# The last fixed expert's loads in a hybrid decoder layer: waiting for the issue of the first gather instead of its landing

## What is computed

```python
h = rms_norm(x, norm_ffn_gain[l])
...
group_p = softmax(t @ w_router_group + b_router_group)
gp, gi = lax.top_k(group_p, 1)
sel = take_along_axis(exp_logits, gi)
ev, ei = lax.top_k(softmax(sel), TOP_K)      # two experts of one group
for e in range(N_EXPERTS):
    hid = silu(t @ w_expert_gate[e]) * (t @ w_expert_up[e])
    out = out + combine[:, e:e + 1] * (hid @ w_expert_down[e])
```

## Time and profile before

| what | us |
|---|---|
| median of 3 runs | 771.15 (770.96 to 771.22) |
| the profiled execution's own time | 771.41 |
| its span, first to last instruction | 769.7 |
| start of the first gather on POOL | 485.13 |
| first transposition of gathered rows on PE | 492.10 |
| last down product on PE starts | 739.71 |

### The profile page before, as it was taken

How to read it: one execution, slowest core, us unless ns; L and a number is a source line. 1 busy time by engine, 2 the same in 40 slices (tenths; PEclk the granted TensorE clock), 3 DMA queues, 4 the chain that set the end, 5 groups by cost and what they waited for, 6 DMA issues and landing times.

```text
span 769.7 us, 10989 instructions
## 1 busy us (share of the span) xinstructions
PE 699.7 (91%) x4246; PEld 512.5 (67%) x4246; DVE 335.4 (44%) x615; ACT 292.1 (38%) x537; POOL 199.5 (26%) x171
## 2 busy tenths in 40 slices
PE   4999999998999999999999996699999999997940
PEld 3688888887887798888777885454445555454520
DVE  4349897989776422465479136600000000000008
ACT  6322656473354643654544033021222222222123
POOL 2044443332151141433453000212122221211110
PEclk9999999999999999999999997699999999999985
DMA  7904333040030030214941248999999999999827
GB/s 232 339 39 164 110 110 109 2 151 15 14 138 14 1 111 2 70 42 165 381 145 57 77 169 342 376 374 394 418 399 418 396 419 397 419 417 419 339 95 280
DMA packets 45330, 164.66 MB, mean 214 GB/s; under 512 B 9500, under 2 KB 13612, under 8 KB 32478
## 3 DMA queue, kind: packets, MB, share of 16 engines
q1 hardware_dynamic: 39966, 155.52, 52.4%
q0 software_dynamic: 5312, 8.42, 3.1%
HBM read 154.09 MB, written 19.53 MB: 226 GB/s over the span
## 4 chain that ended last, share of the span: by engine, by line
PE 83%; DVE 5%; ACT 4%; issue 3%; DMA 2%; POOL 1%; DVEq 0%; SPq 0%; POOLq 0%; ACTq 0%
PE bank L970 14%; PE bank L472 13%; PE bank L474 13%; PE bank L473 13%; PE bank L1004 7%; PE bank L967 5%; PE bank L945 3%; PE bank L998 2%; PE bank L600 2%; PE bank L981 2%; PE bank L863 1%; PE bank L631 1%; PE bank L621 1%; PE bank L803 1%; PE bank L788 1%
## 5 line engine op out<-in xcount | busy, mean ns | idle before, releaser
L1264 POOL TENSOR_TENSOR w_lo<-arena,w_hi 128x1024 fp32r<-128x1024 f32 x36 | 86.1, 2396 | 211.5 <-ACT w_hi L1427 211.5
L472 PE MATMUL bank<-h_hi,w_hi 128*128 128x512 f32 x320 | 128.3, 401 | 0.4 <-DVE arena L1977 0.4
L474 PE MATMUL bank<-h_hi,w_lo 128*128 128x512 f32 x320 | 125.0, 391 | 0.0
L473 PE MATMUL bank<-h_lo,w_hi 128*128 128x512 f32 x320 | 124.6, 389 | 0.0
L970 PE MATMUL bank<-arena 128*64 128x256 f32 x896 | 105.6, 390 | 7.9 <-issue 7.1
L970 PEld LDWEIGHTS bank<-arena 128*64 128x64 f32 x896 | 65.1, 140 | 38.3 <-issue 8.5
L2344 DVE TENSOR_TENSOR arena<-arena,bank 64x256 f32<-64x256 f32 x28 | 11.5, 412 | 180.1 <-ACT arena L1778 180.1
L1889 DVE SCALAR_TENSOR_TENSOR bank<-arena,bank 128x512 f32<-128x512 f32 x116 | 78.7, 749 | 0.1
L1388 POOL DMA_INDIRECT y_rows<-arena,row_half x28 | 28.0, 1000 | 165.0 <-ACT arena L1799 153.5
L474 PEld LDWEIGHTS bank<-h_hi,w_lo 128*128 128x128 f32 x320 | 60.1, 188 | 13.1
L472 PEld LDWEIGHTS bank<-h_hi,w_hi 128*128 128x128 f32 x320 | 60.1, 188 | 12.9 <-DVE arena L1977 0.6
(11 more groups left out here) (361 smaller groups left out, 1136.6 us busy)
## 6 DMA issues: line engine op xcount, KB each, us to landing
arena<-in_w_expert_down_dram SPq DMA_DIRECT2D x33, 1024.0 KB, 20.6
arena<-in_w_expert_gate_dram SPq DMA_DIRECT2D x33, 1024.0 KB, 17.9
arena<-in_w_expert_up_dram SPq DMA_DIRECT2D x33, 1024.0 KB, 21.6
arena<-in_w_in_dram SPq DMA_DIRECT2D x8, 2048.0 KB, 8.1
arena<-in_x_dram SPq DMA_DIRECT2D x8, 512.0 KB, 7.6
arena<-in_w_in_dram SPq DMA_DIRECT2D x4, 1024.0 KB, 10.6
y_rows<-arena SPq DMA_DIRECT2D x8, 512.0 KB, 10.1
arena<-in_w_out_dram SPq DMA_DIRECT2D x2, 2048.0 KB, 11.0
```

The lines of the kernel that those rows point to most:

```text
L472: pe.matmul(o, wh, xh, start=first, stop=False)
L473: pe.matmul(o, wh, xl, start=False, stop=False)
L474: return pe.matmul(o, wl, xh, start=False, stop=last)
L1264: gp.tensor_tensor(as_raw(w_lo[pslot(s)], s), raw(s), as_raw(w_hi[pslot(s)], s).bitcast(F32), ALU.subtract)\
```

## The change

SP waits for an eleventh count of `rconst` instead of the first gather's landing. That count is given by a no-op which POOL executes right after it has issued the first gather and before it issues the second.

```diff
@@ SP
             expert_dn(fixed[0], 0)
-            wait(sp, "ld_h0", 16)
+            wait(sp, "rconst", 11)
             expert_gu(fixed[1], 1)
             expert_dn(fixed[1], 1)
             wait(sp, "sorted", 1)
@@ POOL
             for g in range(NHS):
                 gather(g)
+                if g == 0:
+                    gp.engine_nop().then_inc(S["rconst"], 1)
```

## The result

| | before | changed |
|---|---|---|
| median, us | 771.71 (15 runs, 768.66 to 773.19) | 773.40 (15 runs, 770.52 to 776.71) |
| ratio | | 1.0033, 95% interval 1.0018 to 1.0049 |
| the profiled execution, us | 771.41 | 772.47 |

Slower by 0.33%, 2.5 us by the ratio, 1.7 us by the medians. The forecast was +1.7 us. So the third digit of these ratios is soft, and most of what follows is read from the traces.

What follows compares the result with a forecast made beforehand. The prediction took the weight stream to bound the kernel, through a refill that follows PE. Terms: 0 (no-op) + 0 (idle stretch) + 1.8 (gather) - 0.1 = +1.7 us, giving 772.9 us, range 770.9 to 774.5.

Steps and rivals of the forecast that it cites:

- What bounds the kernel: Expert stage: the weight stream sets the end, hanging on its last refill, which hangs on how early PE got through step 0.
- The wait removed: On SP: expert 1's three loads are issued some 5.6 us earlier, at about 486.4; worth nothing for expert 1 itself.
- The no-op: On POOL ahead of the second gather: delays it by 0 to 0.3 us, taken as 0.1, covered; counted as 0.
- The idle stretch, 0: DMA engines, 491 to 494 us: the change fills 1.3 us of unused time, worth 0 on the path to the end.
- The gather, +1.8 us: First gather: sharing the DMA engines with a full q1, it lands 1.8 us later; bounds 0 to 3.4 us.
- The estimate of 2.5 us: First gather: by the round-robin rule, 8 packets per engine each wait 0.31 us for a load packet; sum would be 773.6.
- TensorE's clock stands at 0.50 from 485 to 494 either way, and I count nothing for it.: PE around the first gather: the half clock is the same before and after the change, so the term is 0.
- -0.1 us absorbed on the way: From the gather to the end: 0.1 us of the delay is taken off; between 0 and 0.4 us could be absorbed.
- The rival of a gather that is hardly delayed: First gather: landing and end move by only 0 to 1 us, giving 771.2 to 772.1 us; chance 0.32.
- that of a gain from the stream: Weight stream: closing the earlier hole moves it forward by up to 1.3 us, typically 770.5 us; chance 0.08.

Runs made afterwards that it cites:

- refill_late: Kernel before, with one more wait on SP: the extra step's down load waits for step 2's gate and up product; ratio to before 1.0051.
- half_packets: Changed kernel, with expert 1's matrices loaded in six 512 KB halves, so load packets are 4 KB and not 8 KB; ratio to before 0.9999.
- behind_third: Changed kernel, with POOL's no-op behind the third gather, so expert 1's loads are issued later; ratio to before 0.9998.
- before_again: The kernel before, timed once more with no edit; ratio to before 0.9987.
- after_again: The changed kernel, timed once more with no edit; ratio to before 1.0018.
- warm8: Kernel before, with 8 dummy matmuls on PE while it waits for the first gather; ratio to before 0.9985.
- warm_after: Changed kernel, with 12 dummy matmuls on PE while it waits for the first gather; ratio to before 0.9986.
- dn0_held: Kernel before, with expert 0's down load also held until the first gather's landing, 1 MB less in q1; ratio to before 0.9993.
- no_wait: Changed kernel, with SP's wait before expert 1's loads removed, so they are issued 12 to 14 us before the first gather; ratio to before 1.0018.
- warm: Kernel before, with 14 dummy matmuls on PE while it waits for the first gather; ratio to before 1.0020.
- warm_all: Kernel before, with 20 dummy matmuls in PE's wait for the first gather and 40 ahead of its wait for the one-hot matrix; ratio to before 1.0031.

## Why the prediction was right, and where it was not

- *What bounds the kernel.* The weight stream sets the end and the stream's refill follows PE: held. Of the 14 traces, twelve have 227 to 229 us from refill to last product, while the refill itself moves by over 4 us. The exceptions are refill_late (225.3), in which only the refill and two loads behind it are late, and half_packets (226.7). Behind it stands the idle time of the DMA engines: the last product follows it within 1.9 us in all 14 traces.
- *The wait removed.* SP issued 1.18 us after the gather's issue, predicted about 1.3. Held.
- *The no-op.* The second gather came 1.42 us after the first in both traces. Held: its cost is nothing.
- *The idle stretch, 0.* Held in the changed kernel: the engines' idle time moved to 498 to 500 us, and there is 2.8 us more of it in all, by the table, as the refill is late. Where the gather is not delayed as well (behind_third), the last product came 1.06 us earlier, of which 0.6 us is an earlier refill, and its idle time is 2.4 us against 2.8 and 2.3 in the two traces of before; so the closed stretch is worth at most some 0.5 us, and no timing shows it.
- *The gather, +1.8 us.* Measured +1.64 and, against each other in the repeated kernels, +1.95. Held, and by the mechanism named, the sharing with q1: half_packets halved the packet and gave back 1.0 us. The size was taken from the median of the later gathers and not worked out, so that it fits to 0.2 us is in part luck. The estimate of 2.5 us was too high. It took one row as the unit in which the engines change queue, which no run shows, and all 8 rows per engine as newly shared, while the first of them moved before expert 1's loads came in.
- *"TensorE's clock stands at 0.50 from 485 to 494 either way, and I count nothing for it."* This step failed. I looked at the clock up to 494 and not at when it comes back: it came back later, 5.8 us after PE's start instead of 4.1, and the first product took 5.52 us instead of 4.72. The term is +0.8 us. It repeats: by the timeline that product takes 4.76 us in before_again and 5.67 in after_again.
- *-0.1 us absorbed on the way.* 2.45 us at the refill became 2.33 at the last product. Held.

The sum by the trace is 1.64 + 0.82 - 0.12 = 2.3 us where I had 1.7; the ratio says 2.5 (1.4 to 3.8), and for after_again 1.4 (0.2 to 2.5). That the medians differ by just the 1.7 us of the forecast is therefore in part luck: a term was missing, and the timing is too coarse to show it. The rival of a gather that is hardly delayed is out, by two traces of the changed kernel; that of a gain from the stream too. The absolute times that I had named for the changed trace hold only when counted from G: the last product was to start at 735.1, which is G + 250.0 in the trace before, and started at G + 250.60; in absolute time it stood at 733.44, as the routing of that execution ran 2.3 us ahead.

## What to carry to other kernels

A transfer that an engine waits for shares the DMA engines with whatever else is queued, here with as many packets for the one queue as for the other, so large load packets beside a gather of small rows make it slow whether they were issued before or after it. Hold the bulk loads back so that their packets come when the small transfer's have moved, which lets their issue stand well before it lands: here an issue 3.8 us behind the gather's cost nothing and one 1.2 us behind it cost 1.6. And ask in how many microseconds the DMA engines will stand idle in all; the end followed that number more closely than any single start. When an engine starts later, look at the granted clock behind its start too, and at how far the stream behind it has slack, since a load held back must still be carried.

## What I had not expected of the hardware

- The time at which TensorE's clock comes back depends on what PE did in the wait: with PE idle from 488 to 492 us it was back at 496.2 (11.1 us after the gather's issue) in before, and 14.4 us after it in the changed kernel; with PE busy on dummy products in the gap, 7.5 us after it in warm8 and 6.7 in warm_after. But it does not simply follow the length of the gap. From its fall in the routing to its return the half clock lasted 24 us in before, with 4.1 us idle, and also in dn0_held, with 1.6 us idle; it lasted 27 us in the changed kernel, with 5.8 us idle, and also in half_packets, with 4.8. So dn0_held's earlier PE start was spent on a product of 5.51 us. What decides between the two lengths, these runs don't show.
- Behind a full q1, no packet of the gather moves in the first 3.5 us after its issue (4.0 in no_wait). With 1 MB less in q1 it was 1.5 us. What the gather waits for in this time is open.
- In 13 of the 14 traces the clock drops again near the end, behind a wait of 2.0 to 2.7 us for weights, and one product takes 5.0 to 5.4 us instead of 3.67. In the changed kernel's trace it hit the last but one (725.71 above), and the next wait shrank to 0.28 us, so it cost nothing. The exception is no_wait, with waits of 2.7 and 2.0 us there too. In warm, warm_all, refill_late, half_packets and warm_after it hit the last as well, where nothing follows that could take it up. How often it hits the last, and whether an edit in mid-kernel can shift it, I have not tested; it may be part of the spread between executions and of warm's 0.2%. Another part is where the routing ends: leaving out warm_all, which held it up, the gather's issue stands between 482.8 and 486.2 us in these traces, and 2.1 us apart in the two traces of the changed kernel.
- Issuing the loads 2.6 us later was enough to free the gather of them fully (8.5 to 6.6 us), since their packets move some 2 us after their issue. Where between 1.2 and 3.8 us the price ends was not tried.
